# Recurrent levels of a two-block layer kernel: differences, exponentials and key products over both halves of each block at once

## The reference

```python
b = jnp.cumsum(gc, axis=2)                       # running sum of log gates within a chunk
diff = b[:, :, :, None, :] - b[:, :, None, :, :]
decay = jnp.exp(jnp.where(tri[:, :, None], diff, -jnp.inf))
att = jnp.einsum('bhtk,bhsk,bhtsk->bhts', qc, kc, decay)
...
state = (jnp.exp(b_last[:, :, 0, :])[..., None] * state
         + jnp.einsum('bhsk,bhsv->bhkv', kc * jnp.exp(b_last - b), vc))
```

## Time and profile before

| | us |
|---|---|
| median of 3 runs (3382.36 to 3388.52) | 3386.4 |
| profiled execution | 3385.07 |
| its span | 3383.6 |
| PE busy | 3097.3 (92%) |
| DVE busy | 1908.9 (56%) |
| ACT busy | 909.4 (27%) |
| POOL busy | 1904.5 (56%) |
| chain that ended last | PE 61%, DVE 28%, ACT 5% |

### The profile page before, as it was taken

How to read it: one execution, slowest core, us unless ns; L and a number is a source line. 1 busy time by engine, 2 the same in 40 slices (tenths; PEclk the granted TensorE clock), 3 DMA queues, 4 the chain that set the end, 5 groups by cost and what they waited for, 6 DMA issues and landing times.

```text
span 3383.6 us, 39580 instructions
## 1 busy us (share of the span) xinstructions
PE 3097.3 (92%) x15146; PEld 2404.3 (71%) x15146; DVE 1908.9 (56%) x2809; ACT 909.4 (27%) x1435; POOL 1904.5 (56%) x1860
## 2 busy tenths in 40 slices
PE   8889989989999889899999999998889898798897
PEld 5677767768777778677787677776677776586675
DVE  6755786751385569676217533335788888512313
ACT  5222213430232220243203232323343333301102
POOL 5555556547675546555567655554455555276461
PEclk9999999999999999899999999999999999999997
DMA  5222222133222222211432222221112122232221
GB/s 192 88 94 94 75 75 75 63 117 125 100 100 89 98 75 89 73 63 66 154 112 89 85 72 78 76 77 66 63 63 75 63 75 75 85 112 87 71 92 59
DMA packets 61069, 294.55 MB, mean 87 GB/s; under 512 B 5680, under 2 KB 10672, under 8 KB 31440
## 3 DMA queue, kind: packets, MB, share of 16 engines
q1 hardware_dynamic: 36384, 247.48, 20.8%
q10 hardware_dynamic: 24496, 44.54, 3.8%
HBM read 274.10 MB, written 16.84 MB: 86 GB/s over the span
## 4 chain that ended last, share of the span: by engine, by line
PE 61%; DVE 28%; ACT 5%; issue 2%; POOL 2%; DMA 1%; DVEq 0%; ACTq 0%; POOLq 0%
PE bank L396 52%; DVE bank L1908 5%; DVE h_lo L1664 2%; DVE rec_ex L2249 1%; DVE rec_cum L2206 1%; POOL w_lo L2430 1%; DVE bank L1735 1%; PE bank L735 1%; DVE rec_small L2235 1%; PE bank L752 1%; PE bank L744 1%; PE bank L924 1%; DVE last_z L2378 1%; POOL w_hi L2428 1%; DVE newton L1643 1%
## 5 line engine op out<-in xcount | busy, mean ns | idle before, releaser
L396 PE MATMUL bank<-h_hi,w_lo 128*128 128x512 f32 x3712 | 1529.0, 412 | 85.7 <-DVE h_lo L1664 34.9
L396 PE MATMUL bank<-h_lo,w_hi 128*128 128x512 f32 x3712 | 1472.6, 397 | 0.0
L396 PE MATMUL bank<-h_hi,w_hi 128*128 128x512 f32 x3712 | 1472.3, 397 | 0.0
L2428 POOL TENSOR_SCALAR w_hi<-w_raw 128x512 fp32r<-128x512 f32 x928 | 675.2, 728 | 1339.3 <-PE bank L396 1279.8
L2430 POOL TENSOR_TENSOR w_lo<-w_raw,w_hi 128x512 fp32r<-128x512 f32 x928 | 1252.2, 1349 | 77.4
L396 PEld LDWEIGHTS bank<-h_hi,w_lo 128*128 128x128 f32 x3712 | 714.9, 193 | 315.0 <-issue 51.7
L396 PEld LDWEIGHTS bank<-h_hi,w_hi 128*128 128x128 f32 x3712 | 712.5, 192 | 156.7
L396 PEld LDWEIGHTS bank<-h_lo,w_hi 128*128 128x128 f32 x3712 | 714.2, 192 | 152.3 <-issue 12.8
L965 ACT ACTIVATE raw<-bank 128x512 f32<-128x512 f32 x148 | 88.5, 598 | 383.5 <-PE bank L396 353.6
L1908 DVE SCALAR_TENSOR_TENSOR bank<-cfm_up,par,bank 128x512 f32<-128x512 f32 x232 | 175.4, 756 | 8.3
L2066 DVE TENSOR_TENSOR xT<-bank,xT 128x512 f32<-128x512 f32 x32 | 22.1, 691 | 221.7 <-PE bank L396 221.0
(11 more groups left out here) (335 smaller groups left out, 2875.3 us busy)
## 6 DMA issues: line engine op xcount, KB each, us to landing
w_raw<-in_wall SPq DMA_DIRECT2D x230, 1024.0 KB, 4.9
x_scratch<-xT ACTq DMA_DIRECT2D x12, 1024.0 KB, 4.9
xT<-x_scratch ACTq DMA_DIRECT2D x12, 1024.0 KB, 7.4
ssd_abc<-acs_scratch ACTq DMA_DIRECT2D x16, 512.0 KB, 3.5
first_xin<-in_x SPq DMA_DIRECT2D x4, 1024.0 KB, 10.7
out<-last_rows ACTq DMA_DIRECT2D x4, 1024.0 KB, 4.2
w_raw<-in_wall SPq DMA_DIRECT2D x8, 256.0 KB, 10.2
raw<-in_wpp ACTq DMA_DIRECT2D x16, 128.0 KB, 2.6
```

The lines of the kernel that those rows point to most:

```text
L396: mm = t.matmul(bank[BANK[u]][:, :], w[:, CS16[k]], h[:, k, :], start=(k == 0 and w is m.w_lo[b]), stop=(k == KT - 1 and w is m.w_hi[b] an ...
L2428: g.tensor_scalar(m.w_hi[b][:, part], m.w_raw[b][:, part], 1.0, 1.0, ALU.mult, ALU.mult).then_inc(*s.hi.inc(u, n))
```

## The change

DVE's `decays` makes one subtraction per direction over whole blocks, 128x512, instead of four over halves. It always subtracts the edge from the running sum. With that the lower halves come out with the opposite sign. The output pattern of `halves` sends the two halves of each block to different rows of `rec_ex`: row 0 now holds the exponents of the keys, row 1 those of the queries. ACT takes one exponential over the lower halves of both rows with scale -1 and one over the upper halves with scale 1, 128x512 each; the second waits for the first as all ACT operations here wait for the one before. DVE's `level` multiplies the keys in one operation, 128x512, reading the lower halves of `rec_kd` from row 0 and the upper ones from row 1. The change is in these lines:

```diff
+def halves(ap, row, h, step):
+    return bass.AP(ap.tensor, ap.offset + row * T, [ap.ap[0], [2 * h, T // (2 * h)], [step * T + h, 2], [1, h]])
...
 ACT
         def decays(j, n):
-            ex = q.ex[n % 2]
+            h, ex = HALVES[n], q.ex[n % 2]
             a.wait_ge(*dve.at("diff", j, n))
-            a.wait_ge(*act.now())
-            a.activation(ex[:, :, :], ex[:, :, :], ACT.Exp).then_inc(*act.inc("decay", j, n))
+            for half, scale in ((0, -1.0), (1, 1.0)):
+                at = ex[:, :, :].rearrange("p r (m x) -> p r m x", x=2 * h)[:, :, :, half * h:half * h + h]
+                a.wait_ge(*act.now())
+                a.activation(at, at, ACT.Exp, scale=scale).then_inc(*act.inc("decay", j, n))
...
 DVE
-            for o, x, y in ((dst(0)[:, :, :, up], wide(0, 1)[:, :, :, up], edge(0)),
-                            (dst(0)[:, :, :, lo], edge(1), wide(1, 0)[:, :, :, lo]),
-                            (dst(1)[:, :, :, lo], edge(0), wide(0, 1)[:, :, :, lo]),
-                            (dst(1)[:, :, :, up], wide(1, 0)[:, :, :, up], edge(1))):
+            for d in range(2):
+                of = q.cum[:, d, :, 1 - d:P + 1 - d].rearrange("p c (n x) -> p c n x", x=2 * h)
+                edge = q.cum[:, d, :, h:P + 1:2 * h].unsqueeze(3).to_broadcast([P, NC, P // (2 * h), 2 * h])
                 v.wait_ge(*dve.now())
-                v.tensor_tensor(o, x, y, ALU.subtract).then_inc(*dve.inc("diff", j, n))
+                v.tensor_tensor(halves(ex[:, :, :], d, h, 1 - 2 * d), of, edge, ALU.subtract).then_inc(*dve.inc("diff", j, n))
...
-                v.tensor_tensor(q.lq[b][:, :], ex[:, 0, :], q.qs[:, :], ALU.mult).then_inc(*dve.inc())
+                v.tensor_tensor(q.lq[b][:, :], ex[:, 1, :], q.qs[:, :], ALU.mult).then_inc(*dve.inc())
                 v.wait_ge(*dve.now())
-                v.tensor_tensor(kk[:, :, lo], ek[:, :, lo], k0[:, :, lo], ALU.mult).then_inc(*dve.inc())
-                v.wait_ge(*dve.now())
-                v.tensor_tensor(kk[:, :, up], ek[:, :, up], k1[:, :, up], ALU.mult).then_inc(*dve.inc("lev", j, n))
+                v.tensor_tensor(halves(q.lk[b][:, :], 0, h, 0), halves(ex[:, :, :], 0, h, 0),
+                                halves(kd[:, :, :], 0, h, 1), ALU.mult).then_inc(*dve.inc("lev", j, n))
```

More of the change, by code:

```diff
@@ L2257, in level @@
                 ex = q.ex[b]
-                part = lambda t: t.rearrange("p (a b) -> p a b", b=2 * h)
-                lo, up = slice(0, h), slice(h, 2 * h)
-                ek, k0, k1, kk = part(ex[:, 1, :]), part(kd[:, 0, :]), part(kd[:, 1, :]), part(q.lk[b][:, :])
                 v.wait_ge(*act.at("decay", j, n))
                 v.wait_ge(*dve.now())
-                v.tensor_tensor(q.lq[b][:, :], ex[:, 0, :], q.qs[:, :], ALU.mult).then_inc(*dve.inc())
+                v.tensor_tensor(q.lq[b][:, :], ex[:, 1, :], q.qs[:, :], ALU.mult).then_inc(*dve.inc())
                 v.wait_ge(*dve.now())
-                v.tensor_tensor(kk[:, :, lo], ek[:, :, lo], k0[:, :, lo], ALU.mult).then_inc(*dve.inc())
-                v.wait_ge(*dve.now())
-                v.tensor_tensor(kk[:, :, up], ek[:, :, up], k1[:, :, up], ALU.mult).then_inc(*dve.inc("lev", j, n))
+                v.tensor_tensor(halves(q.lk[b][:, :], 0, h, 0), halves(ex[:, :, :], 0, h, 0),
+                                halves(kd[:, :, :], 0, h, 1), ALU.mult).then_inc(*dve.inc("lev", j, n))
             else:
```

## The result

| us | before | after |
|---|---|---|
| median of 5 runs | 3386.4 (3382.36 to 3388.62) | 3368.76 (3366.9 to 3370.97) |
| span of the profiled execution | 3383.6 | 3367.3 |
| head 0 / heads 1 to 6 / head 7 | 65.0 / 457.0 / 47.4 | 60.9 / 447.4 / 44.2 |
| PE idle in heads 1 to 6 | 37.1 | 32.7 |
| time at 1.2 GHz in heads 1 to 6 | 30.7 | 17.1 |

The ratio is 0.9948, with a 95% interval of 0.9934 to 0.9963: 17.6 us less, where 21.4 were forecast (3365 from 3386.4). A head is counted here from PE's `far` to the next, head 7 to `combine`.

What follows compares the result with a forecast made beforehand. VectorE was taken to pace heads 0 and 7, and the chain from `hq`'s eviction to `far` to absorb the middle heads' waits. Savings 4.7 + 12.9 + 4.0 = 21.6 us from 3385.07 give 3363.5, plus 1.3, so 3365; range 3352 to 3378.

Steps and rivals of the forecast that it cites:

- Differences and keys: Per level: differences 1.84 to 1.44 us quiet, 4.34 to 2.7 beside POOL; keys 0.92 to 0.72 quiet, 2.1 to about 1.0.
- the rule of 16-byte lines: SBUF accesses in a row must share a 16-byte line for full rate; the new differences at h = 1 jump 2 KB.
- the 0.53 of that rival: Level 6, h = 1: single-element jumps add 0.53 us to each of three operations, 1.6 in all; 3368, chance 0.08.
- My bound of 0.85 for a quiet difference: Upper bound for one quiet 128x512 difference, from two old operations in one; 0.69 us was taken, over 0.85 meant wrong.
- Exponentials: Every level: one of 1.06 us becomes a pair of 1.30, 0.24 more, mostly beside VectorE's work but on the path at level 4.
- Head 0: First head, paced by VectorE: savings at levels 0, 1 and 4 and the waits of levels 5 and 6, sum 4.7 us.
- The term of 2.7 for the waits of levels 5 and 6: Head 0: PE's waits of 1.08 us at level 5 and 1.59 at level 6 both go.
- 0.2 + 0.7 + 1.1: Head 0 savings in us: keys at level 0, a quiet VectorE cycle at level 1, the shorter wait at level 4.
- Head 7: Last head, paced by VectorE: 4.0 us gained at `combine`, not below 2.8 nor above 6.
- Heads 1 to 6: Middle heads: level 4's wait falls 1.78 to 0.65, level 6's 2.82 moves to `far` as 3.6; 12.9 us saved.
- 6 x 74.3: Six middle heads of 74.3 us (44.05 to the eviction of `hq`, 30.24 on to `far`), less 1.7: 444.1 against 457.0.
- The rival of more: Chain from the eviction of `hq` to `far` stays at 27.8 us, six heads save 15 more: 3350, chance 0.12.

Runs made afterwards that it cites:

- e2: The changed kernel with one exponential of 1024 columns per level instead of two of 512, leaving out the signs and so the decays' values: 3365.2 us, ratio 0.9933.
- e5: The changed kernel with POOL's burst after the gate unit of heads 1 to 6 held until VectorE's six small products for `far` are done: 3376.66 us, ratio 0.9965.
- e3: The changed kernel with the old form (four differences, one exponential, two key products) at level 6 alone: 3372.63 us, ratio 0.9957.
- e4: The changed kernel with ScalarE's logarithms ahead of the query's eviction, and two late evictions before level 0's exponential: 3357.99 us, ratio 0.9912.
- e9: The changed kernel with the six small products for `far` on ScalarE instead of VectorE: 3346.65 us, ratio 0.9885.
- e8: The changed kernel with the new form at levels 0 to 2 only and the old form at levels 3 to 6: 3376.34 us, ratio 0.9972.
- e12: The changed kernel with ScalarE's logarithms first, and the small products and four `q.diag` copies on ScalarE: 3323.48 us, ratio 0.9815.

## Why the prediction was right, and where it was off

**Differences and keys.** Right in the size that mattered: quiet 0.69, a contended pair 2.68, level 4's wait 0.55 for 0.65. At h = 1 the rule of 16-byte lines in the Trainium skill, "SBUF — State Buffer", section "Door 1: The DMA port swizzle (why `[64,N]` ≈ `[32,N]`)", agrees with the trace in direction. The jump adds 0.41 to a difference of 0.69, not the 0.53 of that rival, and the keys' product, which reads one of its inputs so, takes 0.81 in place of 0.69. At h = 2, two elements to a place, it costs nothing. My bound of 0.85 for a quiet difference, past which I would be wrong, is broken at this one level of seven. I had given it 0.08. The equal medians that I set against it were of all levels together, and such a row can't show one level of seven. It shows on the path in heads 0 and 7. In the middle heads PE waits 0.96 at level 6, where I had nothing, and 0.8 less at `far`, 2.81 rather than 3.6. With this wait and the 2.57 at level 5 of head 0 the key waits stay at 25.1 us where I had about 15.

**Exponentials.** 1.30 foreseen, 1.29 measured at most levels and 1.37 to 1.40 for h of 2 and 1. e2 puts the whole price at about 2.8 us, which is no more than the spread of its runs.

**Head 0**: 4.7 forecast, 4.1 measured, and here the sum is near by luck. The term of 2.7 for the waits of levels 5 and 6 gave 0.7: from the start of PE's level 4 to the end of its level 7 it takes 11.45 instead of 12.14 us. Level 5's wait grew from 1.08 to 2.57. Level 6's went, but a slow stretch of the clock (2371.4 to 2374.8) stands there now; in e5, which has none in that place, level 6 waits 1.0. VectorE's difference of level 6 and the product behind it, before and after:

```profile
2366.16 4.30 DVE L2249 TENSOR_TENSOR rec_ex<-rec_cum 128x256 f32<-128x256 f32 x4
2370.59 0.69 DVE L2263 TENSOR_TENSOR rec_lq<-rec_ex,rec_qs 128x512 f32<-128x512 f32 x1
```

```profile
2363.83 3.37 DVE L2250 TENSOR_TENSOR rec_ex<-rec_cum 128x512 f32<-128x512 f32 x2
2367.33 1.43 DVE L2261 TENSOR_TENSOR rec_lq<-rec_ex,rec_qs 128x512 f32<-128x512 f32 x1
```

The pair saves 0.9, not the 1.6 that I had, and the query product then stands beside what is left of the burst and loses 0.7 of it again. PE in turn comes 1.6 earlier than I had, because the slow stretch of the clock behind level 4 (2366.8 to 2370.2 before) is gone. What made up for it is the clock too: the way from `far` to level 4 got 3.4 us shorter where I had 0.2 + 0.7 + 1.1, and a slow stretch behind level 1 (2353.2 to 2356.6 before) went there, for which I had no term.

**Head 7**: 4.0 and 3.2, within its bounds of 2.8 to 6. PE reaches level 0 1.0 earlier, level 2 0.9 and level 3 1.5, as forecast. The last pair is 0.4 dearer than its old form, as e3 shows.

**Heads 1 to 6**: 12.9 forecast, 9.6 measured. The mechanism was right. The level waits shrank (1.78 to 0.55, 2.82 to 0.96), the wait came at `far` in all of them, and the chain from the eviction of `hq` to `far` took 30.6 at the ends of heads 1 to 5 and 31.3 at that of head 6 (30.2 foreseen). Heads 2, 3 and 4 take 74.5 each against 74.3, and head 1 72.5 against 72.6. The term that was mis-sized is "6 x 74.3". Head 5 takes 76.1 and head 6 75.3. Head 6 ends in a wait of 3.59 for `far` instead of 2.81. In head 5 no slow stretch follows the wait for `far`, so that PE runs ahead of ScalarE and waits 1.78 for the eviction of the value unit (the projection at 2705.27, shown above); the slow stretch comes behind that, from 2705.9. In heads 3 and 4 the clock falls right behind `far`, and the same eviction is waited for 0.46 or less. I had no term for this wait. In e2 it is 1.55, ScalarE's 0.24 less, no slow stretch follows, and head 5 takes 73.9 like the others. That the 0.24 made the difference was not tried apart.

**The rival of more** (chain at 27.8, 3350) falls: the chain took 30.6. e4 shows that an earlier start doesn't shorten it. Quiet small products do, in e5 to 27.0 to 28.2, but there the wait came back at level 0; taking them off VectorE (e9) shortened it further and left only 0.8 to 1.3 at level 0 in the middle heads.

**The path of the gain** was right in its total, and the clock's part stood in the sum without my naming it. By the trace more than half of the middle's gain is clock: 5.2 of 9.6 as less PE busy time. My 74.3 was put together from two measured pieces, head 4 up to the eviction, which holds one slow stretch, and head 3 from the eviction on, which holds none. Less the one of head 1 that makes five slow stretches, as many as there are now, where the kernel before had nine. That those behind level 4 in heads 1, 3 and 6 and those behind level 6 would go I did not argue. And one of the five stands elsewhere than I had it, behind the eviction in head 5. By my own sizes of the waits (0.65 and 3.6 in each of six heads) the idle time would have fallen by some 8.6 us, an estimate from the waits of before; it fell by 4.4, since 0.96 stayed at level 6 and ScalarE's eviction came in. e8 shows the clock's share best: 6.1 of its 8.2 us are busy time.

**What stays open**: which waits let the clock fall. From head 1 on, in the two kernels, 11 of the 12 waits of 2.8 to 3.6 at `far` and level 6 (up to the entry of head 7) are followed by a slow stretch; 1.76 to 1.79 at level 4 of before is in three heads of six, 1.59 in the same place of e8 in none of six, 0.55 in none. The length of the last wait doesn't decide it alone: waits of 0.94 at level 6 and 0.57 at level 7 are followed by a slow stretch in no middle head of the changed kernel, but in three of six in e9 and in e12.

## What to carry to other kernels

Where VectorE works beside a burst of POOL, count VectorE's operations rather than their columns: use fewer and longer ones (4.34 us for four halves, 2.68 for two wholes), or put the small ones on ScalarE. When a wait of the bounding engine is removed, price the chain to the next join first. Here it moved from level 6 to `far`, and from `far` to level 0 when a burst was held, and most of it left only with the work. Price each wait with what the clock does after it: here up to 1.7 us for each slow stretch that no longer follows. And look at the duration of a new pattern at its extreme stride by itself, since the median of the group hid it.

## What the runs showed of the hardware

- A 128x512 float32 subtraction on VectorE whose output alternates between two rows of a tile after every element takes 1.10 us; after every second element or more, 0.69. A multiplication that reads one input so takes 0.81.
- Six 128x128 `tensor_scalar` operations on VectorE take 5.6 us together beside a POOL burst and 2.0 without one. The same on ScalarE take 0.40 each with or without one.
- POOL held back by a semaphore (e5) began 0.2 us after the operation that it waited for and cost VectorE in the next stretch (12.3 us instead of 8.8) what it had spared in the last (2.0 instead of 5.6).
- The clock fell to 1.2 GHz after PE waits of 1.76 to 1.79 in three heads of six, and in none after waits of 1.59 in the same place of another version (e8). A stretch of 3.4 us held 10 matmuls instead of 17.
